# An RWKV scan: inverse levels taken head by head, filler matmuls moved from behind the growths to behind the lower products

## The reference

```python
def rwkv7_scan(r, decay, k, v, kk, a, s0, reverse):
    xs = tuple(jnp.moveaxis(t.astype(jnp.float32), 1, 0) for t in (r, decay, k, v, -kk, kk * a))

    def step(s, inp):
        r_t, w_t, k_t, v_t, a_t, b_t = inp
        sa = jnp.einsum('bhvk,bhk->bhv', s, a_t)
        s = s * w_t[:, :, None, :] + sa[..., None] * b_t[:, :, None, :] + v_t[..., None] * k_t[:, :, None, :]
        return s, jnp.einsum('bhvk,bhk->bhv', s, r_t)

    s_last, ys = lax.scan(step, s0, xs, reverse=reverse)
    return jnp.moveaxis(ys, 0, 1), s_last

def rwkv7_mixer(hx, hc, p, v_first_x, v_first_c, ctx_out):
    ...
    for z in range(2):
        dc, kdc, ac = rwkv7_direction(kc, wlc, alc, p, z)
        dx, kdx, ax = rwkv7_direction(kx, wlx, alx, p, z)
        yc_z, s_ctx = rwkv7_scan(rc, dc, kdc, vc, kkc, ac, s0, z == 1)
        yx_z, _ = rwkv7_scan(rx, dx, kdx, vx, kkx, ax, s_ctx, z == 1)
        ...
```

## Time and profile before

| | us |
|---|---|
| median of three runs | 2485.53 |
| lowest, highest | 2484.59, 2487.69 |
| the profiled execution | 2488.11 |
| its span, first to last instruction | 2486.3 |
| PE busy | 2415.5 (97%) |
| DVE busy | 1338.3 (54%) |
| ACT busy | 790.2 (32%) |
| POOL busy | 748.4 (30%) |
| the scan's pairs 0 to 15, with the layer's end | 91.4 to 1032.3 |

### The profile page before, as it was taken

One profiled execution on the slowest core, in us unless ns is written; L12 is line 12 of the kernel. 1 busy time (PEld: TensorE's weight loads), 2 busy tenths in 40 slices (PEclk: granted clock), 3 DMA queues, 4 the chain that ended last, 5 costly groups with the idle time before them and its releaser, 6 DMA issues.

```text
span 2486.3 us, 65623 instructions
## 1 busy us (share of the span) xinstructions
PE 2415.5 (97%) x28580; PEld 1775.9 (71%) x28580; DVE 1338.3 (54%) x2764; ACT 790.2 (32%) x1612; POOL 748.4 (30%) x730
## 2 busy tenths in 40 slices
PE   6999999999999998899999999999999999999998
PEld 1566666666666666658888888865558888875797
DVE  4766666666666665454563333834624434545553
ACT  3354544445454443221221121013510014022312
POOL 2533433343434442100001034400055400540381
PEclk9999999999999999899999999999999999999999
DMA  7111111111111113544336732220134444332343
GB/s 302 49 39 45 42 39 48 41 46 39 39 39 39 50 37 124 188 169 153 136 133 213 269 120 89 91 84 30 43 130 171 146 145 139 136 120 72 98 153 110
DMA packets 80148, 258.30 MB, mean 104 GB/s; under 512 B 11639, under 2 KB 16984, under 8 KB 79096
## 3 DMA queue, kind: packets, MB, share of 16 engines
q1 hardware_dynamic: 75304, 242.94, 28.5%
q0 software_dynamic: 1360, 5.89, 0.7%
q10 hardware_dynamic: 3200, 5.27, 0.6%
HBM read 253.02 MB, written 1.05 MB: 102 GB/s over the span
## 4 chain that ended last, share of the span: by engine, by line
PE 55%; DVE 2%; DMA 1%; ACT 0%; issue 0%; SPq 0%; DVEq 0%; ACTq 0%
PE ps L2327 9%; PE ps L2125 9%; PE ps L2050 9%; PE ps L1975 7%; PE ps L2180 4%; PE ps L2105 3%; PE ps L2376 2%; PE ps L2225 2%; PE ps L2393 1%; PE ps L1895 1%; PE ps L2245 1%; PE ps L2210 1%; PE ps L2265 1%; PE ps L2204 1%; DMA ring<-in_w_mods 1%; PE ps L2083 1%
## 5 line engine op out<-in xcount | busy, mean ns | idle before, releaser
L2050 PE MATMUL ps<-h,ring 128*128 128x256 f32 x1024 | 225.6, 379 | 0.0
L2050 PEld LDWEIGHTS ps<-h,ring 128*128 128x128 f32 x1024 | 193.9, 190 | 34.9 <-issue 9.9
L1053 ACT ACTIVATE general<-general 64x512 f32<-64x512 f32 x160 | 101.8, 636 | 164.8 <-DVE general L1252 162.2
L583 PE MATMUL ps<-general,ring 128*128 128x512 f32 x256 | 134.9, 623 | 0.8 <-issue 0.8
L3515 POOL TENSOR_TENSOR general<-h 128x1024 f32<-128x1024 f32 (+1 forms) x4 | 7.2, 1803 | 423.8 <-DVE general L3255 238.0
L599 PE MATMUL ps<-general,ring 128*128 128x512 f32 x256 | 134.1, 629 | 0.0
L774 PEld LDWEIGHTS ps<-general 64*64 64x64 f32 (+1 forms) x5120 | 77.5, 130 | 68.8 <-issue 44.9
L2180 PE MATMUL ps<-ring,h 128*128 128x512 f32 x256 | 110.2, 592 | 0.0
L2327 PE MATMUL ps<-general,ring 128*128 128x256 f32 (+1 forms) x576 | 106.3, 327 | 0.6 <-DVE general L3328 0.6
L3509 POOL TENSOR_TENSOR general<-general 128x256 f32<-128x256 f32 x16 | 12.7, 796 | 310.2 <-ACT general L2550 310.2
L1252 DVE STREAM_TRANSPOSE general<-general 128x512 f32<-128x512 f32 x160 | 104.3, 690 | 2.2
(11 more groups left out here) (440 smaller groups left out, 5329.7 us busy)
## 6 DMA issues: line engine op xcount, KB each, us to landing
ring<-in_w_mods SPq DMA_DIRECT2D x88, 512.0 KB, 4.4
ring<-in_w_feature SPq DMA_DIRECT2D x74, 512.0 KB, 3.2
ring<-in_w_rkvg SPq DMA_DIRECT2D x64, 512.0 KB, 3.7
ring<-in_w_in SPq DMA_DIRECT2D x48, 512.0 KB, 3.2
ring<-in_w_merge SPq DMA_DIRECT2D x48, 512.0 KB, 4.2
ring<-in_w_out SPq DMA_DIRECT2D x32, 512.0 KB, 6.5
ring<-in_w_token SPq DMA_DIRECT2D x24, 512.0 KB, 4.8
ring<-in_w_merge SPq DMA_DIRECT2D x48, 256.0 KB, 2.7
```

Of the source, the lines that this page charges most:

```text
L583: mm = pe.matmul(ps[:, 0, :], W.wt[:, 0, k, :], W.mix_k[:, k, :], start=(k == 0), stop=(k == KD - 1))
L1053: last = act.activation(W.U[g:g + 64, 1], W.X0[a:a + 64, 1], ACT.Copy)
L2050: mm = pe.matmul(ps[:, n % 4, 0:NX], weights(key, k), R.h[:, k, 0:NX], start=(k == 0), stop=(k == KD - 1))
```

## The change

Four things change, all in this stage.

- The loops of `below` and `grow` run head by head (`h` outside, then `j`, `p`, `z`), and their results lie in two PSUM banks for each head. The semaphores `y_done`, `y_out`, `ty_done` and `t_out` count heads and no longer directions, so masks and adds go by head too: a mask is one operation over both directions of one head (256 elements per partition as before), an add of levels 1 to 4 is two operations for each head (128 elements each), four for the level where there were two. The add of level 5 (`add_last`) stays one operation for each direction and waits for both heads.
- A below product waits for the add of its own head, where both directions had to be added.
- `FILL_GROWN` is zero for levels 1 to 4: no piece stands behind these growths.
- `FILL_BELOW` asks for 2200, 1800, 1500 and 1500 columns at levels 1 to 4, where it was 1000 at each. The sums of both tables are 2200, 1800, 1500 and 1500 before as well.

```diff
-FILL_BELOW = (0, 1000, 1000, 1000, 1000, 500)
-FILL_GROWN = (0, 1200, 800, 500, 500, 1000)
+FILL_BELOW = (0, 2200, 1800, 1500, 1500, 500)
+FILL_GROWN = (0, 0, 0, 0, 0, 1000)
...
-    def below(l):
-        for j in range(4):
-            for h in range(2):
+    def below(i, l):
+        for h in range(2):
+            if l > 1:
+                pe.wait_ge(t_out[h], (LAST - 1) * i + l - 1)
+            for j in range(4):
                 for p in range(2):
...
-                        mm = pe.matmul(ps[own, b0 + h, j * P:j * P + 32], left, right, start=True, stop=True)
-                        if (j, h, p) == (3, 1, 1):
-                            mm.then_inc(Z("y_done")[z], 1)
+                        mm = pe.matmul(ps[own, bank, j * P:j * P + 32], left, right, start=True, stop=True)
+            mm.then_inc(Z("y_done")[h], 1)
 
     def grow(i, l):
         for z in range(2):
-            pe.wait_ge(y_out[z], LAST * i + l)
             pe.wait_ge(u_out[z], 6 * i + l)
-        for j in range(4):
-            for h in range(2):
+        for h in range(2):
+            pe.wait_ge(y_out[h], LAST * i + l)
+            if l == LAST:
+                pe.wait_ge(y_out[1], LAST * (i + 1))
+            for j in range(4):
...
-                        if (j, h, p) == (3, 1, 1):
-                            mm.then_inc(Z("ty_done")[z], 1)
+            mm.then_inc(Z("ty_done")[h], 1)
...
         for l in range(1, LAST + 1):
-            if l > 1:
-                for z in range(2):
-                    pe.wait_ge(t_out[z], (LAST - 1) * i + l - 1)
-            below(l)
+            below(i, l)
...
             fill(part, FILL_BELOW[l])
             grow(i, l)
-            fill(part, FILL_GROWN[l])
+            if FILL_GROWN[l]:
+                fill(part, FILL_GROWN[l])
...
+    def mask_level(i, h, l):
+        dve.wait_ge(Z("y_done")[h], LAST * i + l)
+        mask = W.lmask[:, l - 1, :, :].unsqueeze(2).broadcast_to([P, 2, 4, 32])
+        dve.tensor_tensor(W.Y[:, :, 4 * h:4 * h + 4, :], head_banks(h), mask, ALU.mult).then_inc(Z("y_out")[h], 1)
+
+    def add_level(i, h, l):
+        dve.wait_ge(Z("ty_done")[h], LAST * i + l)
+        for z in range(2):
+            dst = half_columns(W.T[:, z, 4 * h:4 * h + 4, :], l, z)
+            grown = head_banks(h)[:, z].rearrange("p q (b w) -> p q b w", w=1 << l)
+            last = dve.tensor_tensor(dst, dst, grown, ALU.add)
+        last.then_inc(Z("t_out")[h], 1)
...
     def turn_inverse(i, l):
         for z in (1, 0):
             if l == 1:
                 dve.wait_ge(Z("eye_out")[z], i + 1)
             else:
-                dve.wait_ge(Z("t_out")[z], (LAST - 1) * i + l - 1)
+                for h in range(2):
+                    dve.wait_ge(Z("t_out")[h], (LAST - 1) * i + l - 1)
```

More of the change, by code:

```diff
@@ L786, in grow @@
                     for z in range(2):
-                        b0, g, q = 2 + 2 * z, solved_in(z, p), 4 * h + j
+                        g, q = solved_in(z, p), 4 * h + j
                         if l < LAST:
-                            mm = pe.matmul(ps[a:a + 64, b0 + h, j * P:j * P + 32], W.U[g:g + 64, z, q, :], W.Y[g:g + 64, z, q, :],
+                            mm = pe.matmul(ps[a:a + 64, 2 + 2 * h + z, j * P:j * P + 32], W.U[g:g + 64, z, q, :], W.Y[g:g + 64, z, q, :],
                                            start=True, stop=True)
@@ L794, in grow @@
                             own = slice(g + t, g + t + 32)
-                            mm = pe.matmul(ps[g + c:g + c + 32, b0 + h, j * P:j * P + 32], W.Y[own, z, q, :], W.U[own, z, q, t:t + 32],
+                            mm = pe.matmul(ps[g + c:g + c + 32, 2 + 2 * z + h, j * P:j * P + 32], W.Y[own, z, q, :], W.U[own, z, q, t:t + 32],
                                            start=True, stop=True)
-                        if (j, h, p) == (3, 1, 1):
-                            mm.then_inc(Z("ty_done")[z], 1)
+            mm.then_inc(Z("ty_done")[h], 1)
     def seen_values(i):
@@ L1225, in mask_tokens, with head_banks, add_last @@
             dve.tensor_tensor(W.Ax[:, z, h].rearrange("p (j q) n -> p j (q n)", q=2), src, mask, ALU.mult).then_inc(Z("xm_out")[z], 1)
-    def mask_level(i, z, l):
-        dve.wait_ge(Z("y_done")[z], LAST * i + l)
-        mask = W.lmask[:, l - 1, z, :].unsqueeze(1).broadcast_to([P, 8, 32])
-        dve.tensor_tensor(W.Y[:, z], two_banks(2 + 2 * z)[:, :, 0:32], mask, ALU.mult).then_inc(Z("y_out")[z], 1)
-    def add_level(i, z, l):
-        dve.wait_ge(Z("ty_done")[z], LAST * i + l)
-        grown = two_banks(2 + 2 * z)[:, :, 0:32]
-        if l < LAST:
-            dst = half_columns(W.T[:, z], l, z)
-            dve.tensor_tensor(dst, dst, grown.rearrange("p q (b w) -> p q b w", w=1 << l), ALU.add).then_inc(Z("t_out")[z], 1)
-        else:
-            dve.wait_ge(Z("u_out")[z], 6 * i + LAST)
-            t = 32 - 32 * z
-            dst = W.U[:, z, :, t:t + 32]
-            dve.scalar_tensor_tensor(dst, grown, W.lmask[:, LAST - 1, 1 - z, 0:1], dst, ALU.mult, ALU.add).then_inc(Z("u_out")[z], 1)
+    def head_banks(h):
+        return ps[:, 2 + 2 * h:4 + 2 * h, :].rearrange("p z (j n) -> p z j n", n=P)[:, :, :, 0:32]
+    def mask_level(i, h, l):
[9 more added lines that the diff above has]
+        last.then_inc(Z("t_out")[h], 1)
+    def add_last(i, z):
+        for h in range(2):
+            dve.wait_ge(Z("ty_done")[h], LAST * i + LAST)
+        dve.wait_ge(Z("u_out")[z], 6 * i + LAST)
+        t = 32 - 32 * z
+        dst = W.U[:, z, :, t:t + 32]
+        grown = two_banks(2 + 2 * z)[:, :, 0:32]
+        dve.scalar_tensor_tensor(dst, grown, W.lmask[:, LAST - 1, 1 - z, 0:1], dst, ALU.mult, ALU.add).then_inc(Z("u_out")[z], 1)
     def turn_inverse(i, l):
@@ L1344, in pairs_dve @@
             turn_inverse(i, l)
-            for z in range(2):
-                mask_level(i, z, l)
+            for h in range(2):
+                mask_level(i, h, l)
             if l == 1:
@@ L1360, in pairs_dve @@
                 floor(m)
-            for z in range(2):
-                add_level(i, z, l)
+            if l < LAST:
+                for h in range(2):
+                    add_level(i, h, l)
+            else:
+                for z in range(2):
+                    add_last(i, z)
         if ahead:
```

2 lines of the change are left out of this document (1 added, 1 removed).

## The result

| | before | after |
|---|---|---|
| median of five runs, us | 2485.16 | 2494.2 |
| lowest, highest | 2484.03, 2487.69 | 2489.68, 2499.57 |
| the profiled execution | 2488.11 | 2494.2 |
| its span | 2486.3 | 2492.4 |

A forecast was written before the change was run, and what follows sets the result against it. TensorE's queue was taken as the bound: 14 x (1.64 - 1.47 + 0.55 - 0.15) = 8.0 us, pair 0 0.0, pair 15 -1.0, together +7.0 on 2485.53, forecast 2492.5 us, range 2483 to 2502.

The forecast's parts named there:

- Saved switches: TensorE, first below product to solve: seven filler runs instead of twelve, five switches at 0.30 us, 1.47 us a pair saved.
- Four new seams: Levels 1 to 4: below product waits for its head's add, 1.37 us against 0.96, 0.41 a seam, 1.64 a pair.
- Rival B: Dearer seams: a head's two adds run one behind the other, 11.5 us over 64 seams, 2504.0 us; chance 0.08.
- No second wait: At a seam, head 1's below product could start at 1.84 us, just when head 0's is through: no further wait.
- The turns: Turns L655, L657 move ahead of growth 2 and wait for GpSimd's normalisation L1477: 0.55 us a pair, 14 times.
- rival A: No wait at the turns: L1477 takes 0.61 us, total 2484.8; decided by a wait under 0.41 us; chance 0.17.
- The state phase: GpSimd's product L1462 comes later and VectorE's L1191 starts first: -0.15 us a pair, between -0.40 and 0.
- The sum of a pair: Pairs 1 to 14: 1.64 - 1.47 + 0.55 - 0.15 us a pair, 8.0 us for the fourteen.
- Pair 15: Weight load's end does not move; two early products leave the path, blocks moved up run slower: -1.0 us, -2.0 to 0.
- Behind the solve: ScalarE's first two solution copies done at solve + 4.9 us, own states needing them at solve + 5.32: no cost.
- growth l + 1: Could start 3.90 us behind growth l; seam, below product and three pieces end at 5.20, so no wait.
- rivals C and D: C: no state-phase gain, 2494.6 us, chance 0.12. D: late copy of v costs 0.33 a pair, 2497.1 us, chance 0.08.

The follow-up runs named there:

- one_later: Loops by heads with the tables of the kernel before, but 1100 columns asked for behind growth 1 instead of 1200; 2478.51 us, ratio 0.9969.
- tables_bare: Kernel before with the new tables alone, no piece taken where the table has a zero; 2532.79 us, ratio 1.0184.
- phase_bad: Kernel after plus instructions of satisfied waits, 99 a pair and 16 ahead of the scan, putting borders late in small-block strings; 2706.31 us.

## Why the prediction was right, and where it was not

- **Saved switches, 1.47 us a pair.** Right. The levels took 29.30 where 28.98 is the same work in the old order: +0.32, and less the waits below (1.24, 0.16, 0.35), 1.43 were saved; this is a difference, not a row. one_later shows one switch alone at 0.30.
- **Four new seams, 1.64.** Mechanism right, size too large: 1.28 at levels 2 to 4 and 1.24 at level 1, and not 1.37, 1.24 a pair. The first add started 0.74 behind the growth as forecast (0.73); the failed step is TensorE's start 0.15 behind the adds' end, which I took from a product that follows a longer operation: here it is 0.05, in tables_bare, behind adds of 256 elements, 0.15 (487.14 to 487.29). Rival B is out: the second add starts 0.21 behind the first, which lasts 0.29.
- **No second wait.** Right at levels 2 to 4, wrong at level 5, where the columns are half as many and head 0's product is through before head 1's add: 0.85 and not 0.69, 0.16 a pair. I had worked it out for a full block and let it stand for all.
- **The turns, 0.55.** 0.35. L1487 starts when I said, but the scan beside it stood 0.2 us earlier, and it took 0.81. In rival A it would have taken 0.61. The wait is still below the 0.41 that I had named as the mark of A, so the case lies between A and the forecast.
- **The state phase, -0.15.** -0.23 or so, and L1189 is back at 0.68. Right.
- **The sum of a pair** was therefore +0.09 and not +0.57: 1.3 us and not 8.0 for the fourteen.
- **What the sum lacked.** Stalls at instruction borders, and the clock that falls behind some: +7.7 us in pairs 1 to 14 and +3.5 in pair 0, for which I had written 0.0. It filled the gap that the mis-sized terms left. That the fourteen periods came out at 58.51, where I had named 58.4 as the sign of being right, is this coincidence, and so is the total: my errors of +3.5 us in pair 0 and -5.1 in pair 15 nearly cancel.
- **Pair 15, -1.0 (-2 to 0).** -6.1 in the profiled execution, and nothing shows that the new order has a part in it: without a wait at the load the old order takes 67.0 to 67.1 us, the new 67.9 to 69.0. The step that failed is that the load ends a chain that does not move: its end moves by 5 us between executions (30.6 to 35.3). TensorE came to it at 31.3 us and no longer at 25.1, behind the landing; with the old order it came between 25.1 and 31.0.
- **Behind the solve, growth l + 1.** Nothing waits there that did not before; rivals C and D are out.

Left open: why the load's chain of five differs from execution to execution, why one stall of 1 us is followed by half the clock and another is not, and why phase_bad had one long stall a pair where three strings end near a border. Taking instructions out of the strings, rather than moving the borders, was not tried.

## What to carry to other kernels

Count instructions, not only microseconds: a stretch of some 200 instructions on TensorE that passes in under 2.5 us can outrun their fetch (here in about half of the cases), and long instructions laid between short ones buy the time for it. Before filler is moved away from a wait, price the switch that is saved (0.30 us here) against the wait that comes to light (0.3), and look for the edit that saves a switch without uncovering anything, as one_later does. And where a wait ends on a chain of loads, take several profiles before a gain or a loss there is given to the change.

## What the runs showed of the hardware

- TensorE's instructions come in packets of 256 (228 packets for 58396). Where a border falls into small blocks with little or no filler between them, TensorE can stop, for 0.2 to 1.6 us: 20 stops in the kernel after, all within two instructions of a border. It goes on 1.2 to 1.5 us behind the end of the packet.
- An instruction that holds only satisfied waits (two of them) takes 0.10 us on TensorE when many stand in a row (20.7 us for 208). It is no cheap padding.
- A stall of 1 us in the midst of busy work can be followed by a granted clock of 0.50 (232.48 in the kernel after: two pieces in 3.60 us and not 1.9), so that a stall can cost up to twice its length again; of four such stalls two had it.
